# A fused two-block kernel: 64 columns per head in one mixer's solve, and inverses with their diagonal 64-blocks stacked

## What is computed

```python
L = jnp.where(strict, jnp.einsum("bhnid,bhnjd->bhnij", kb, k) * decay, 0.0)
rhs = jnp.concatenate([v * beta[..., None], kb * jnp.exp(g)[..., None]], axis=-1)
sol = lax.linalg.triangular_solve(L, rhs, left_side=True, lower=True, unit_diagonal=True)
...
v_new = u_c - w_c @ S
o = qd @ S + a_c @ v_new
S = S * gl + kd.T @ v_new
```

## Time and profile before

| | us |
|---|---|
| three runs, median (lowest, highest) | 1608.83 (1602.46, 1609.0) |
| profiled execution, span | 1608.8 |
| TensorE matmuls busy | 1542.6 (96%) |
| VectorE busy | 1066.1 (66%) |
| ScalarE busy | 732.4 (46%) |
| GpSimd busy | 69.8 (4%) |
| mixer A, inverses and application | 308 to 392 |
| hybrid, four rounds | 1207 to 1343 |

### The profile page before, as it was taken

How to read it: one execution, slowest core, us unless ns; L and a number is a source line. 1 busy time by engine, 2 the same in 40 slices (tenths; PEclk the granted TensorE clock), 3 DMA queues, 4 the chain that set the end, 5 groups by cost and what they waited for, 6 DMA issues and landing times.

```text
span 1608.8 us, 35749 instructions
## 1 busy us (share of the span) xinstructions
PE 1542.6 (96%) x15477; PEld 1482.4 (92%) x15477; DVE 1066.1 (66%) x1285; ACT 732.4 (46%) x814; POOL 69.8 (4%) x51
## 2 busy tenths in 40 slices
PE   7999999999999999999998999999988899999998
PEld 7999999888999999999988999989876778999997
DVE  5776487764776557664677776466767875777446
ACT  5433346543533444333555434364473444555333
POOL 2000000100100010000101000021000000100000
PEclk9999999998999999999999999999999999999999
DMA  8565545201566555555533665654310012555552
GB/s 272 187 201 189 194 148 183 80 3 54 184 199 192 193 192 181 189 188 183 184 106 110 191 197 188 200 181 158 107 51 3 3 56 80 181 186 194 198 187 76
DMA packets 155064, 243.25 MB, mean 151 GB/s; under 512 B 9283, under 2 KB 106174, under 8 KB 154814
## 3 DMA queue, kind: packets, MB, share of 16 engines
q1 hardware_dynamic: 154510, 240.63, 45.6%
q10 hardware_dynamic: 432, 0.79, 0.2%
HBM read 240.34 MB, written 1.05 MB: 150 GB/s over the span
## 4 chain that ended last, share of the span: by engine, by line
PE 88%; DVE 6%; ACT 3%; issue 1%; DMA 1%; POOL 0%; SPq 0%; ACTq 0%; DVEq 0%
PE dense_ps L2498 25%; PE dense_ps L2499 24%; PE dense_ps L2500 24%; PE dense_ps L450 1%; PE mixer_ps L538 1%; PE mixer_ps L450 1%; DVE w_lo L2868 1%; PE mixer_ps L1756 1%; PE mixer_ps L1183 1%; PE mixer_ps L1174 0%; DVE xT L2986 0%; ACT ly_r L595 0%; DMA raw<-in_ffn_w_gu 0%; ACT score_b L1213 0%; ACT w_hi L2695 0%
## 5 line engine op out<-in xcount | busy, mean ns | idle before, releaser
L2868 DVE TENSOR_TENSOR w_lo<-raw,w_hi 128x2048 fp32r<-128x2048 f32 x225 | 523.0, 2336 | 240.0 <-ACT w_hi L2695 239.2
L2498 PE MATMUL dense_ps<-h_hi,w_hi 128*128 128x256 f32 x2368 | 666.2, 281 | 11.9 <-DVE h_lo L2943 8.3
L2499 PE MATMUL dense_ps<-h_lo,w_hi 128*128 128x256 f32 x2368 | 659.6, 279 | 0.0
L2500 PE MATMUL dense_ps<-h_hi,w_lo 128*128 128x256 f32 x2368 | 659.4, 278 | 0.0
L2695 ACT ACTIVATE w_hi<-raw 128x2048 fp32r<-128x2048 f32 x225 | 428.6, 1914 | 331.2 <-DMA raw<-in_ffn_w_down 115.5
L2498 PEld LDWEIGHTS dense_ps<-h_hi,w_hi 128*128 128x128 f32 x2368 | 449.2, 190 | 18.0 <-issue 17.5
L2499 PEld LDWEIGHTS dense_ps<-h_lo,w_hi 128*128 128x128 f32 x2368 | 447.5, 189 | 0.9 <-issue 0.5
L2500 PEld LDWEIGHTS dense_ps<-h_hi,w_lo 128*128 128x128 f32 x2368 | 447.2, 189 | 0.0
L2498 PE MATMUL dense_ps<-g_hi,w_hi 128*128 128x256 f32 x960 | 265.8, 277 | 0.0
L2499 PE MATMUL dense_ps<-g_lo,w_hi 128*128 128x256 f32 x960 | 265.8, 277 | 0.0
L2500 PE MATMUL dense_ps<-g_hi,w_lo 128*128 128x256 f32 x960 | 265.8, 277 | 0.0
(11 more groups left out here) (554 smaller groups left out, 1781.6 us busy)
## 6 DMA issues: line engine op xcount, KB each, us to landing
raw<-in_ffn_w_gu SPq DMA_DIRECT2D x176, 512.0 KB, 4.7
raw<-in_ffn_w_down SPq DMA_DIRECT2D x88, 512.0 KB, 4.1
raw<-in_w_ff SPq DMA_DIRECT2D x64, 512.0 KB, 4.2
raw<-in_w_in SPq DMA_DIRECT2D x36, 512.0 KB, 4.4
raw<-in_a_w_in SPq DMA_DIRECT2D x32, 512.0 KB, 4.4
raw<-in_a_w_out SPq DMA_DIRECT2D x8, 512.0 KB, 4.1
raw<-in_b_w_in SPq DMA_DIRECT2D x8, 512.0 KB, 4.1
raw<-in_b_w_out SPq DMA_DIRECT2D x8, 512.0 KB, 4.0
```

The source lines that it names most:

```text
L2498: pe.matmul(o, hi, mh, start=start, stop=False)
L2499: pe.matmul(o, hi, ml, start=False, stop=False)
L2500: return pe.matmul(o, lo, mh, start=False, stop=stop)
L2868: dve.tensor_tensor(w_lo[:, p % SLOTS, :], raw[:, p % SLOTS, :], w_hi[:, p % SLOTS, :].bitcast(F32), ALU.subtract).then_inc(lo_ready, 1)
```

## The change

Three things. **The stacked inverse:** `x`, `xt` and `y` become tiles with 64 columns for each matrix. The upper diagonal 64-block lies on partitions 0 to 63 and the lower one on partitions 64 to 127, in the same columns; products write PSUM in the same way. The copies by ScalarE and the merges by VectorE have half the elements. The number of products is the same.

**The whole matrix** that the application needs is put together in a tile of its own (`inv_w`, 128 columns for each matrix). GpSimd zeroes it once. After level 5 VectorE waits for `inv_up` and copies the diagonal blocks of xt in two instructions (one per half of the partitions); in the hybrid these are half of the matrices, and GpSimd copies the diagonal blocks of x for the other half, in two instructions (`diagonal_pool`), for which `solve(0)` waits on `diag_kept`. Level 6 writes its block directly into `inv_w`. Level 0's merge of xt takes each half of the partitions by itself where it reads the matrix.

**The hybrid's application:** each product with 128 moving columns becomes two with 64 weight columns and 64 moving columns, one for each half of the output partitions. `w_sys` has 64 columns per product, u is copied by one instruction instead of two, `s_bd` by one instruction for each half of the partitions. The hybrid has one set of `x_r` and `xt_r` for all rounds; ScalarE writes the identities for the next round in `apply(i)`, behind the first `w_sys`, when `diag_kept` and `inv_up` allow it.

```diff
+    ("strict_up", P), ("neg_low", P), ("ident_half", 64), ...
-MASK_PARTS = [..., ("merge", (LEVELS - 1) * 64), ("merge_t", (LEVELS - 1) * 64)]
+MASK_PARTS = [..., ("merge", (LEVELS - 1) * 32), ("merge_t", (LEVELS - 1) * 32)]
...
+    def half_columns(ap):
+        return ap[:, :, 0:64]
+    def diagonal(nt_of):
+        return lambda s_, a: nt_of(s_)[a, a]
+    def stacked(x):
+        return lambda s_, a: x[a, s_, :]
+    def quads(pe, to, half, lhs, rhs):
         for s4 in range(4):
-            for q in range(2):
-                p_ = slice(64 * q, 64 * q + 64)
-                end_ = pe.matmul(bank[p_, P * s4 + 64 * q:P * s4 + 64 * q + 64], lhs(4 * half + s4)[p_, p_],
-                                 rhs(4 * half + s4)[p_, p_], start=True, stop=True)
+            for a in (UP, LOW):
+                end_ = pe.matmul(to[a, s4, :], lhs(4 * half + s4, a), rhs(4 * half + s4, a), start=True, stop=True)
...
-                act.activation(y[:, 4 * half:4 * half + 4, :], banks(half, 1), ACT.Copy).then_inc(y_kept, 1)
+                act.activation(y[:, 4 * half:4 * half + 4, :], bank_half(half), ACT.Copy).then_inc(y_kept, 1)
...
+                if lv == LEVELS - 1:
+                    dve.tensor_copy(whole_t[UP, h4, LOW], bank_half(half, D_ps)[UP]).then_inc(inv_up, 1)
+                    continue
...
+            if lv == LEVELS - 2:
+                dve.wait_ge(inv_up, 14 * batch + 2 * lv + 2)
+                for a in (UP, LOW):
+                    dve.tensor_copy(whole_t[a, :, a], xt[a, :, :])
             beside(lv)
...
+    def diagonal_pool(pool, parts, batch):
+        pool.wait_ge(x_up, 12 * batch + 2 * (LEVELS - 2) + 2)
+        for k, (to, of) in enumerate(parts):
+            pool.tensor_copy(to, of).then_inc(diag_kept, 1)
+            pool.wait_ge(diag_kept, diag_count(batch + 1) - len(parts) + k + 1)
...
+            if lv == LEVELS - 2:
+                dve.wait_ge(inv_up, 14 * batch + 2 * lv + 2)
+                for a in (UP, LOW):
+                    dve.tensor_copy(by_four(whole, NEED_R[1], a, a), by_four(xt, NEED_R[1], a, UP))
             beside(lv)
...
                 if phase == 0:
+                    pe.wait_ge(diag_kept, diag_count(GROUPS_A + i + 1))
                     for half in range(2):
                         pe.wait_ge(inv_up, 14 * (GROUPS_A + i) + 13 + half)
                 for h in range(2):
                     for d in range(2):
                         s_ = 4 * h + 2 * d + (d if phase == 0 else 1 - d)
-                        last = pe.matmul(M_ps[:, 1, P * (2 * h + d):P * (2 * h + d) + P], (xt_, x_)[d][:, s_, :],
-                                         w_sys[:, 2 * h + d, :], start=True, stop=True)
+                        for a in HALVES:
+                            last = pe.matmul(of_head(M_ps, 1, a, h, d), inv_w[:, s_, a], w_sys[:, 2 * h + d, :],
+                                             start=True, stop=True)
...
             for d in range(2):
-                o_ = D_ps[:, 0, P * d:P * d + P]
-                pe.matmul(o_, bk_tok[:, d, 0, :], u_tok[:, 0, d, :], start=True, stop=False)
-                last = pe.matmul(o_, bk_tok[:, d, 1, :], v_tok_r[:, d, :], start=False, stop=True)
+                for x, of_tok in enumerate((u_tok[:, 0, d, :], v_tok_r[:, d, :])):
+                    for a in HALVES:
+                        last = pe.matmul(D_ps[a, 0, 64 * d:64 * d + 64], bk_tok[:, d, x, a], of_tok[:, a],
+                                         start=d + x == 0, stop=d + x == 2)
...
             for phase in range(2):
                 act.wait_ge(r_w, 2 * i + phase + 1)
-                act.activation(w_sys[:, :, :], banks(0, 1) if phase else banks(2, 1, D_ps), ACT.Copy).then_inc(r_wk, 1)
-            if i and i + 1 < RT:
-                act.activation(XT_R[(i + 1) % 2][:, :, :], over_mid(ident, 8), ACT.Copy).then_inc(r_init, 1)
+                act.activation(w_sys[:, :, :], of_heads(*((M_ps, 0) if phase else (D_ps, 2))),
+                               ACT.Copy).then_inc(r_wk, 1)
+                if phase == 0 and i + 1 < RT:
+                    act.wait_ge(diag_kept, diag_count(GROUPS_A + i + 1))
+                    act.wait_ge(inv_up, 14 * (GROUPS_A + i + 1))
+                    act.activation(x_r[:, :, :], over_mid(constant("ident_half"), 8), ACT.Copy)
+                    act.activation(xt_r[:, :, :], over_mid(constant("ident_half"), 8), ACT.Copy).then_inc(r_init, 1)
...
-            dve.tensor_copy(u_tok[:, phase, :, 0:64], u_[:, 0, :, 0:64])
-            dve.tensor_copy(u_tok[:, phase, :, 64:128], u_[:, 1, :, 64:128]).then_inc(r_uk, 1)
+            dve.tensor_copy(u_tok[:, phase, :, :].rearrange("p d (h i) -> p h d i", h=2),
+                            of_heads(M_ps, 1).rearrange("p (h d) i -> p h d i", h=2)).then_inc(r_uk, 1)
...
-                last = dve.scalar_tensor_tensor(out=s_bd[:, d, :], in0=D_ps[:, 0, P * d:P * d + P],
-                                                scalar=small_r[:, 32 + 4 * d + i:33 + 4 * d + i], in1=ones_head,
-                                                op0=ALU.mult, op1=ALU.mult)
+            for a in HALVES:
+                last = dve.tensor_tensor(s_bd[a, :, a], D_ps[a, 0, 0:P].rearrange("p (d i) -> p d i", d=2),
+                                         whole[a].unsqueeze(2).to_broadcast((64, 2, 64)), ALU.mult)
```

More of the change, by code:

```diff
@@ new lines, in inverse_dve @@
+                dve.copy_predicated(out=blocks(x[:, h4, :], lv, 0), mask=merge_mask("merge", lv),
+                                    data=blocks(bank_half(half), lv, 0)).then_inc(x_up, 1)
+                if lv:
+                    end_ = dve.copy_predicated(out=blocks(xt[:, h4, :], lv, 1), mask=merge_mask("merge_t", lv),
+                                               data=blocks(bank_half(half, D_ps), lv, 1))
+                else:
+                    for a in (UP, LOW):
+                        end_ = dve.copy_predicated(out=blocks(xt[a, h4, :], lv, 1), mask=merge_mask("merge_t", lv)[a],
+                                                   data=blocks(nt_of(half)[a, :, a], lv, 1))
@@ L539, in crossed @@
         return end_
     def inverse4_pe(pe, nt_of, x, xt, y, ready, batch, beside, between):
-        low, up = slice(64, P), slice(0, 64)
+        nt, x_, xt_, y_ = diagonal(nt_of), stacked(x), stacked(xt), stacked(y)
         for lv in range(LEVELS):
@@ L596, in inverse4_act, with inverse4_dve @@
             beside(lv)
-    def inverse4_dve(dve, nt_of, x, xt, batch, beside):
+    def inverse4_dve(dve, nt_of, x, xt, whole, batch, beside):
         for lv in range(LEVELS):
             for half in range(2):
+                h4 = slice(4 * half, 4 * half + 4)
                 if lv == 0:
@@ new lines, in inverse4_dve @@
+                dve.copy_predicated(out=blocks(x[:, h4, :], lv, 0), mask=merge_mask("merge", lv),
+                                    data=blocks(bank_pair(half), lv, 0)).then_inc(x_up, 1)
+                mask_ = merge_mask("merge_t", lv)
+                if lv:
+                    dve.wait_ge(zt_mm, turned)
+                    end_ = dve.copy_predicated(out=blocks(xt[:, h4, :], lv, 1), mask=mask_,
+                                               data=blocks(bank_half(half, D_ps), lv, 1))
+                else:
+                    to = xt[:, h4, :]
+                    for a in (UP, LOW):
+                        dve.copy_predicated(out=blocks(to[a, 0:2], lv, 1), mask=mask_[a, 0:2],
+                                            data=blocks(nt_of(half)[a, :, a], lv, 1))
+                    end_ = dve.copy_predicated(out=blocks(to[:, 2:4], lv, 1), mask=mask_[:, 0:2],
+                                               data=blocks(bank_half(half, D_ps)[:, 2:4], lv, 1))
@@ L713, in second_values @@
             for h in range(HG):
[L714 removed]
+                last = pe.matmul(to[:, h, :], SET_A[g]["inv_w"][:, 2 * h + 1, :], rest[:, h, :], start=True, stop=True)
             last.then_inc(a_v1, 1)
@@ L1471, in build @@
     v_tok_r = m.take("v_tok_r", [P, NB, P])
-    w_sys = m.take("w_sys", [P, 4, P])
+    w_sys = m.take("w_sys", [P, 4, 64])
+    m.at += 4 * 64 * 4
     u_tok = m.take("u_tok", [P, 2, 2, P])
```

236 lines of the change are left out of this document (114 added, 122 removed).

## The result

The kernel after takes 1623.61 us (median of 20 runs, 1610.33 to 1632.96), the kernel before beside it 1609.72 (20 runs, 1601.06 to 1627.04). The ratio is 1.0057, with a 95% interval from 1.0034 to 1.0079: slower by about half a percent, where 0.8% faster was forecast. The ratio is formed from the fast executions of both kernels run side by side, so it is not the quotient of the two medians. The profiled execution has a span of 1613.2 us (time 1614.94) against 1608.8. It is one of the shorter ones of the kernel after, so the two traces differ by less than the kernels do.

What follows compares the result with a forecast made beforehand. Applications were taken as bound by TensorE, inverses as a latency chain with TensorE and VectorE nearly full. Terms 7.75 + 4.0 + 3.0 - 1.8 - 0.75 + 0.3 gave 12.5 us: 1608.8 to 1596.3 us, range 1588 to 1605.

Steps and rivals of the forecast that it cites:

- Application: Hybrid's four rounds: products in 64-column halves overlap, gaining 1.9, 1.5, 1.5 and 2.85 us, 7.75 us in all.
- rival (a): Hybrid's application: halves do not overlap at 64 columns; total gain only 5.5 us, 1603.3 us; chance 0.12.
- y copies and merges: Both mixers' inverses: half-size ScalarE copies gain 19 x 0.21 = 4.0 us, VectorE's level 1 merges 3.0 us.
- Added copies on VectorE: After level 5, hybrid rounds 0 to 2: two diagonal copies start quarter 0 0.6 us later each, -1.8 us.
- Rival (b): VectorE's added copies are cheap and the rest hides better: 17 us gained, 1591.8 us; chance 0.12.
- the low end: VectorE's two added copies after level 5 cost 0.4 us, 0.2 apart, the lower bound against 0.67.
- GpSimd's copies: Ahead of the hybrid's first solve: two 64x256 diagonal copies, 0.8 to 1.8 us with waits, hidden within some 3.5 us.
- Rival (e): Another wait (GpSimd's copies, ScalarE's order) takes half of the gain: 1602 us; chance 0.14.
- Rival (d): Hybrid: TensorE's clock falls in emptier applications; short fall costs 4 us (1600), long up to 31 (1627; chance 0.04).
- Mixer A: Its two inverses: shorter y copies and level 1 merges, -0.75 us for added copies, 0.3 for the last merge.
- Rival (c): Inverse levels 1 to 5: stacked blocks writing the same bank columns take turns, 74 us slower, 1671 us; chance 0.03.

Runs made afterwards that it cites:

- e1: Kernel after with 128 bytes per partition left free behind the masks, so operands keep the addresses of the kernel before: 1605.06 us, ratio 0.9941 to before.
- e17: Kernel after with everything moved up 128 bytes, what lies behind the masks 128 more (weights at 0, moving operands at 192): 1608.45 us, ratio 0.9926 to before.
- e5: Kernel before with only the hybrid's application in groups of 64 columns, inverses and operand places unchanged: 1610.57 us, ratio 0.9989 to before.
- e2: Kernel before with everything behind the masks moved by 128 bytes: 1626.93 us, ratio 1.0070 to before.
- e18: Kernel before with everything moved up 128 bytes, weights too (weights at 0, moving operands at 192): 1617.08 us, ratio 1.0004 to before.
- e7: Kernel after ended behind its first feed-forward block, everything behind the masks moved up 64 bytes: 218.0 to 218.9 us.
- e11: Kernel after ended behind its first feed-forward block, everything behind the masks moved up 160 bytes: median 216.6 us.
- e12: Kernel after ended behind its first feed-forward block, everything behind the masks moved up 96 bytes: median 216.7 us.
- e14: Kernel after ended behind its first feed-forward block, everything behind the masks moved up 32 bytes: median 220.1 us.
- e15: Kernel after ended behind its first feed-forward block, everything behind the masks moved up 224 bytes: median 214.9 us.
- e16: Kernel after at the old operand places with the hybrid's application back in 128 columns, so stacked inverses alone: 1607.26 us, ratio 0.9961 to before.

## Why the prediction was wrong

**The step that failed** stands twice in it: "The change touches none of the dense products", and "The stages behind follow their mixers directly: their first products wait for the mixers' results, so the gain is kept". The first sentence is true of the instructions and false of their time. The change moved their moving operand by 128 bytes against the weights, and this made the 117.8-ns cadence so much more likely that the dense stages lost more (15.3 us in the profiled pair) than the mixers gained. The profiled pair is mild: with a ratio of 1.0057, some 9 us, and 8 to 12 us gained in the mixers, the usual loss is some 17 to 21 us (an estimate). The prediction says "The masks are smaller, the memsets on GpSimd are early: nothing": the masks were the line of the diff to stop at. The trace of before held the warning. Its dense stages ran at two cadences, 179 and 172 products in 20 us at a clock of 1.00 (740 to 760 us, above), and I had looked only at busy share and clock, which can't show it. None of the five rivals named a change outside the mixers.

With the distance held, the forecast's ratio (1596.3 / 1608.8 = 0.992) lies in the intervals of e1 and e17. By its terms, for the profiled kernel after unless another is named:

- **Application, forecast 7.75 us (1.9, 1.5, 1.5, 2.85).** Right in kind, 10% small inside the applications: e5 shows 8.54 (2.28, 1.82, 1.82, 2.62). Its whole hybrid stretch gained only 4.37, by losses outside them that the forecast had not. The groups of 16 run in 0.46 to 0.61 us from start to start; rival (a), no overlap, is refuted.
- **y copies and merges, 4.0 + 3.0 us for both mixers.** ScalarE's copies take 0.383 us, as said. In the hybrid the inverses came out 1.81, 1.79 and 1.27 us shorter (rounds 1 to 3), and the stretch up to the first application 2.0: 6.9 us, where my terms give 4.3 for it (nine copies at 0.21 and four times 0.6). I had dropped the copies at level 5, since VectorE takes over there; they do shorten the inverse, and the wait comes behind it, in the next term.
- **Added copies on VectorE, -1.8 us in rounds 0 to 2.** Mis-sized: the solve waits 1.15 us longer in each, -3.45. The two copies take 0.77 us; that the rest is what TensorE is earlier at this point is argued, not shown. Against the kernel before it waits 0.71 longer. Rival (b), cheap copies, is refuted by the same wait. Together with the term before it is 3.4 us net, against 2.5. The Trainium skill ("VectorE: DVE Perf Modes", section "Mode 2×_2P — use both read ports for one tensor") lets such a copy run at two elements a cycle. The trace does not show it for this copy: 64x256 took 0.387 us (L656), against 0.418 for the copy of 128x256 from the product's bank (L2312), which this rule does not speed up. The cast of the earlier trace rows, from which I had the low end, took 0.43 for twice as many columns, so it did not carry over.
- **GpSimd's copies, hidden.** Right: done at 1300.7, the solve at 1303.65; its releaser is VectorE. Rival (e), that another wait takes half of the gain, named the wrong engine.
- **Rival (d), the clock.** Came in its short form: 3.4 us at 1.2 GHz in the applications of rounds 0 and 1. They are 0.96 and 1.42 us longer than e5's with the 1.15 added: -2.4 us. e1 has three such stretches and e17 one of 3.4 and one of 6.8 us. The forecast had nothing for them; the rival had 4 us for one short one. A similar stretch in mixer A (346.6 us) stands in e2 and e18 too, which have the mixers of before, so it isn't the change's.
- **Mixer A**, forecast 2.25 us, gained 1.88 with that stretch in it. How much each term gave there was not separated.
- **Rival (c), stacked blocks taking turns.** Refuted: the inverses got shorter, not longer by 74 us.

Hybrid: 8.54 + 6.87 - 3.45 - 2.38 is 9.6, and 9.53 was measured. The sum of the mixers was off by 1.1 us of 12.5 in this pair and by 2.7 on the mean of three executions of each; the sign was set elsewhere. That the sum came so near is in part luck: the terms missed in both directions (6.87 for 4.3, -3.45 for -1.8, -2.38 for nothing).

**What stays open.** Why the distance acts as it does, and what decides in a given execution which cadence a stage draws. In whole kernels a distance of 64 doesn't forbid 113.3 ns (the second and fourth block of the kernel after), nor does 192 forbid 117.8. Why the change shows no gain at the distance 64 is open too. It was not tried whether the distance repeats every 256 bytes, nor whether the one with 120.0 ns would be slow in a whole kernel. VectorE's copy was not moved behind its key work, which would be the next step for e1.

## What to carry to other kernels

An edit that changes the size of anything placed ahead of a hot operand is an edit of that operand's place: pin the hot tensors first, or pad so that their addresses stay, and only then time the idea. When a stage that you did not touch changes its time, count its instructions per microsecond at equal clock; busy share says nothing there. And test a change once with everything else left in place: here one line of padding turned +0.6% into -0.6%.

## What the runs showed of the hardware

- A stream of 128x128 by 128x256 fp32 products, TensorE never idle and its clock at 2.4 GHz, has more than one cadence: 113.3, 116.7, 117.3, 117.8, 118.3, 118.7 or 120.0 ns from start to start, by where the moving operand starts in its partition relative to the weights (ten first-block kernels; e7, e11, e12, e14 and e15 with one profiled execution each); up to 5.9% on every product. Within one kernel's second half the mean over 120 products in a row stays the same to 0.03 ns.
- The Trainium skill ("TensorE: Matmul & The Clock Gate", section "Back-to-back issue gap") gives N / 2.4 + 2.5 ns as the warm gap of an isolated product, an estimate of 109.2 ns for 256 columns. The fastest stream here is at 113.3.
- At a distance of 192 bytes, and of 64, the cadence is 113.3 or 117.8 ns. It can change wherever the stream is broken and differs between executions of the same kernel; 192 draws the fast one far more often (12 of 14 first blocks against 1 of 10). Between two executions of the same code (before and e18) it made 5.9 of 6.2 us.
- Behind a wait of 1.86 us of TensorE in each application of rounds 0 to 2, seven of the nine applications in the kernel after, e1 and e17 had 3.4 or 6.8 us at 1.2 GHz; behind waits of 0.7 to 1.4 us (before, e5, e16) none had. In e5 an idle time of 1.88 us inside the last inverse was followed by 3.4 us at 1.2 GHz too.
